# A hybrid decoder layer on one core: the prologue with rstd in diagonal matrices, state-major tables, and the first product tile begun inside the second half of x

## The reference

```python
xn = rmsnorm(x, norm_g)                       # x * rsqrt(mean(x^2) + 1e-6) * g
proj = xn @ w_in                              # 2048 -> 10240: u_a, z_a, q, k, v, z_b, g_a, g_b
# S5 branch, per group g (64) and state n (64):
dt = exp(log_dt)[:, None]; a_bar = exp(lam * dt)      # lam = A_re + i A_im
b_bar = ((a_bar - 1) / lam) * (B_re + i B_im)
h_t = a_bar * h_{t-1} + b_bar u_t;  y = Re(C h) + D u
# stick-breaking attention on q, k, v; both branches gated, merged, @ w_out, final rmsnorm
```

## Time and profile before

| | us |
|---|---|
| median of 3 runs | 3260.21 |
| lowest, highest | 3258.67, 3263.64 |
| the profiled execution | 3258.7 |
| its span, first to last instruction | 3256.9 |
| PE busy in the span | 3124.3 (96%) |
| DVE, ACT, POOL busy | 1006.6, 997.6, 760.1 |

### The profile page before, as it was taken

The page is one execution under the profiler, slowest core; times in us unless marked ns, Lnnn a source line. Parts: engine busy times, 40 slices in busy tenths (PEclk is TensorE's granted clock), DMA queues, the critical chain, the costliest instruction groups (busy, mean ns, idle before and its releaser), DMA issues.

```text
span 3256.9 us, 50354 instructions
## 1 busy us (share of the span) xinstructions
PE 3124.3 (96%) x20212; PEld 3043.6 (93%) x20212; DVE 1006.6 (31%) x1345; ACT 997.6 (31%) x1258; POOL 760.1 (23%) x2309
## 2 busy tenths in 40 slices
PE   4999999999999999999999999999899999999997
PEld 4999999899999989999998999999899999999997
DVE  5113213311321331132133113212465214332265
ACT  5215313521531352153144215314522101121142
POOL 5550360055036005404600540450012000000000
PEclk8999999999999999999999999999999989999999
DMA  5221222122122212212221221222348545342283
GB/s 151 56 90 58 61 67 80 57 56 92 55 61 68 79 60 57 91 53 62 67 79 61 65 83 53 63 66 79 118 135 272 194 150 176 98 136 71 65 243 107
DMA packets 395720, 304.05 MB, mean 93 GB/s; under 512 B 57250, under 2 KB 364018, under 8 KB 393458
## 3 DMA queue, kind: packets, MB, share of 16 engines
q1 hardware_dynamic: 395506, 301.02, 30.2%
HBM read 227.27 MB, written 65.27 MB: 90 GB/s over the span
## 4 chain that ended last, share of the span: by engine, by line
PE 84%; POOL 5%; ACT 3%; DVE 3%; issue 2%; SPq 1%; DMA 1%; POOLq 0%; DVEq 0%; ACTq 0%
PE acc L1635 71%; PE side L1596 5%; PE side L1775 2%; PE side L1828 1%; PE side L1770 1%; ACT L790 1%; DMA t_oz<-work 1%; ACT stage L790 1%; DVE work L1402 1%; POOL prologue L1039 1%; POOL work L1147 0%; DVE work L1412 0%; POOL work L1149 0%; POOL work L1148 0%; POOL work L1150 0%
## 5 line engine op out<-in xcount | busy, mean ns | idle before, releaser
L1635 PE MATMUL acc<-x_high,w_high 128*128 128x344 f32 (+2 forms) x5440 | 1229.4, 329 | 17.8 <-issue 9.9
L1635 PE MATMUL acc<-x_low,w_high 128*128 128x344 f32 (+2 forms) x5440 | 1186.0, 321 | 0.0
L1635 PE MATMUL acc<-x_high,w_low 128*128 128x344 f32 (+2 forms) x5440 | 1181.6, 321 | 0.0
L1635 PEld LDWEIGHTS acc<-x_high,w_high 128*128 128x128 f32 x5440 | 915.3, 190 | 43.1 <-issue 32.4
L1635 PEld LDWEIGHTS acc<-x_low,w_high 128*128 128x128 f32 x5440 | 928.1, 190 | 0.0
L1635 PEld LDWEIGHTS acc<-x_high,w_low 128*128 128x128 f32 x5440 | 918.5, 189 | 0.0
L1321 DVE TENSOR_TENSOR w_low<-w_raw,w_high 128x1024 fp32r<-128x1024 f32 x233 | 290.7, 1248 | 1052.2 <-ACT w_high L796 1052.1
L796 ACT CAST w_high<-w_raw 128x1024 fp32r<-128x1024 f32 x232 | 243.0, 1047 | 1008.3 <-PE acc L1635 937.1
L1137 POOL COPY work<-s_tables 128x28 f32 x16 | 8.6, 536 | 1385.9 <-DMA work<-t_state_seeds 1385.9
L1596 PE MATMUL side<-work 128*128 128x128 f32 (+6 forms) x832 | 152.7, 308 | 9.7 <-DVE work L1388 9.7
L1596 PEld LDWEIGHTS side<-work 128*128 128x128 f32 (+3 forms) x832 | 100.2, 159 | 43.0 <-issue 25.6
(11 more groups left out here) (287 smaller groups left out, 2517.4 us busy)
## 6 DMA issues: line engine op xcount, KB each, us to landing
w_raw<-in_w_in SPq DMA_DIRECT2D x160, 512.0 KB, 3.8
w_raw<-in_w_out SPq DMA_DIRECT2D x48, 512.0 KB, 4.0
work<-t_sig_ga SPq DMA_DIRECT2D x24, 516.0 KB, 4.5
out<-work SPq DMA_DIRECT2D x18, 512.0 KB
t_sig_gb<-stage SPq DMA_DIRECT2D x16, 516.0 KB, 4.2
t_qk<-stage SPq DMA_DIRECT2D x16, 516.0 KB, 4.9
work<-t_qk SPq DMA_DIRECT2D x16, 516.0 KB, 3.7
t_sig_ga<-stage SPq DMA_DIRECT2D x16, 516.0 KB, 4.2
```

The lines of the kernel that those rows point to most:

```text
L1635: ins = mm(acc[s][:, a, 0:n], w[b][:, kk, :], x[:, kx, c0:c0 + n], start=start, stop=stop)
```

## The change

- DVE no longer scales x. For each row block it writes a 128 x 128 matrix with rstd on the diagonal (`diag`, over the second high weight buffer), and the step on PE is a product of the block's columns with that matrix in place of a transpose.
- log_dt is loaded to all 128 partitions (broadcast) and A_re, A_im ahead of x block 1; PE transposes A right away; time steps, tables and angle are computed on 128 partitions, state-major, and the seven tables are written to `tab` where they are used. The fourteen table transposes, ACT's copy and the semaphores `tp_ready`, `par_t`, `tab_ready` are gone. The denominator moves behind the second pair of norms.
- `first_tile` on PE: after 21 of 32 steps it does the first 344 columns of chunk 0 of the first output tile, one feature tile between two steps; then C's transposes, the last three steps, the S transposes, the other 688 columns of chunk 0, and chunk 1. The steps of the second half use five banks. The loop over i is turned by eight steps.
- ACT and DVE split chunk 0 between the halves; `squares` and `x_high` are interleaved 3, 3, 2 in place of 2, 3, 4.

```diff
+        sp.dma_start(T[3], log_dt[0:1, :].to_broadcast([P, GROUPS])).then_inc(dt_in, 16)
+        sp.dma_start(A_rows[:, 0:64], A_re[0]).then_inc(par_in, 16)
+        sp.dma_start(A_rows[:, 64:128], A_im[0]).then_inc(par_in, 16)
         load_x(1)
-        sp.dma_start(tp[:, 0:64], A_re[0]).then_inc(par_in, 16)
-        sp.dma_start(tp[:, 64:128], A_im[0]).then_inc(par_in, 16)
-        sp.dma_start(tp[:, 128:129], log_dt.rearrange("a g -> g a")).then_inc(par_in, 16)
...
-        for n in range(9, 24):
+        for n in range(8, KT):
             x_high(n)
         act.wait_ge(raw_loaded[0], 16)
         nc.scalar.copy(hi[0][:, :, :], raw[0][:, :, :]).then_inc(hi_ready, 1)
-        for n in range(24, 2 * KT):
+        for n in range(KT, 2 * KT):
             x_high(n)
-        act.wait_ge(par_t, 1)
-        nc.scalar.copy(tab[:, :, :], side[:, 0, 0:7 * GROUPS].rearrange("p (a g) -> p a g", a=7)).then_inc(tab_ready, 1)
         act.wait_ge(seed_mm, 1)
...
-        def scale(n):
-            V.tensor_scalar(x_block(n), x_block(n), nrstd[:, NEW + n:NEW + n + 1], None, ALU.mult).then_inc(x_scaled, 1)
+        def spread(n):
+            V.tensor_scalar(diag[:, n, :], ident[:, :], nrstd[:, NEW + n:NEW + n + 1], None, ALU.mult).then_inc(x_diag, 1)
...
+        def x_transposes(n):
             half, k = n // KT, n % KT
-            if k == 0:
-                pe.wait_ge(x_scaled, 4 * half + 4)
-            if n >= 6:
-                pe.wait_ge(x_lo, n - 5)
+            prior = [m for m in range(n) if X_BANKS[m] == X_BANKS[n]]
+            if prior:
+                pe.wait_ge(x_lo, prior[-1] + 1)
             for b in range(4):
-                last = tr(acc[n % 2][:, n // 2 % 3, b * P:(b + 1) * P], x_block(4 * half + b)[:, k, :], ident[:, :])
+                if k == 0:
+                    pe.wait_ge(x_diag, 4 * half + b + 1)
+                last = one(x_bank(n)[:, b * P:(b + 1) * P], x_block(4 * half + b)[:, k, :], diag[:, 4 * half + b, :])
             last.then_inc(x_tr, 1)
...
+        def first_tile():
+            for n in range(KT + 5):
+                x_transposes(n)
+            acc_free(0, U)
+            split_ready(1)
+            pe.wait_ge(x_lo, KT)
+            for k in range(CK):
+                last_op = products(0, k, k, 0, ALL[0:1], k == 0, False)
+                x_transposes(KT + 5 + k)
+            pe.wait_ge(seed_in, 4 * 16)
+            pe.wait_ge(den_ready, 2)
+            for k in range(FT):
+                last = tr(side_flat[:, k * P:(k + 1) * P], C_in[:, k * P:(k + 1) * P], ident[:, :])
+            last.then_inc(seed_mm, 1)
+            for n in range(KT + 5 + CK, 2 * KT):
+                x_transposes(n)
+            pe.wait_ge(x_lo, 2 * KT)
+            for k in range(4):
+                last = tr(acc[1][:, 2, k * P:(k + 1) * P], S_in[:, k * P:(k + 1) * P], ident[:, :])
+            last.then_inc(seed_mm, 1)
+            for k in range(CK):
+                last_op = products(0, k, k, 0, ALL[1:], k == 0, False)
+            last_op.then_inc(chunk_used, 1)
...
-                            pe.wait_ge(tab_ready, 1)
...
         with pe.Fori(0, FT - 1) as i:
-            phase_a(i, False)
-        phase_a(FT - 1, True)
+            phase_a(i, False, range(8, PTS))
+            phase_a(i + 1, False, range(8))
+        phase_a(FT - 1, True, range(8, PTS))
```

More of the change, by code:

```diff
@@ L733, in _ @@
         act.wait_ge(pre_mm, 1)
-        nc.scalar.copy(gcol[:, :], side[:, 1, 0:KT])
+        nc.scalar.copy(gcol[:, :], side[:, 1, 0:KT]).then_inc(gcol_ready, 1)
         squares(0)
@@ L745, in _ @@
         squares(4)
-        for n in range(2):
+        for n in range(3):
             x_high(n)
@@ L749, in _ @@
         root(2, NEW + 4, NEW + 6)
-        for n in range(2, 5):
+        for n in range(3, 6):
             x_high(n)
         squares(6)
-        for n in range(5, 9):
+        for n in range(6, 8):
             x_high(n)
@@ L1025, in _ @@
         step = Chain(pool, pool_chain, 3)
-        T = [tp[:, 64 * n:64 * n + 64] for n in range(TS)]
-        dt = T[3][:, 0:1]
+        dt = T[2]
         Ar, Ai = T[0], T[1]
@@ L1259, in angle, with split_lo @@
             V.tensor_tensor(q_, hh, hh, ALU.mult).then_inc(den_ready, 1)
-        dve.wait_ge(par_in, 48)
+        dve.wait_ge(dt_in, 16)
         time_steps()
-        step(V.tensor_tensor(den, Ar, Ar, ALU.mult), V.tensor_tensor(part, Ai, Ai, ALU.mult))
-        step(V.tensor_tensor(den, den, part, ALU.add))
-        V.reciprocal(den, den).then_inc(den_ready, 1)
+        dve.wait_ge(par_mm, 1)
+        V.tensor_copy(tp[:, 0:128], side[:, 1, P:2 * P]).then_inc(den_ready, 1)
+        def split_lo(b, n1):
+            dve.wait_ge(hi_ready, n1)
+            V.tensor_tensor(lo[b][:, :, :], raw[b][:, :, :], f32(hi[b][:, :, :]), ALU.subtract).then_inc(lo_ready, 1)
         def norms(b, a, e):
@@ L1290, in _ @@
         V.tensor_tensor(sn, sn, gcol[:, :].unsqueeze(1).broadcast_to([P, NEW, KT]), ALU.mult).then_inc(xs_sq, 1)
-        angle()
         dve.wait_ge(x_sq, 4)
         norms(1, NEW + 2, NEW + 4)
-        scale(2)
-        scale(3)
+        spread(2)
+        spread(3)
+        dve.wait_ge(den_ready, 1)
+        step(V.tensor_tensor(den, Ar, Ar, ALU.mult), V.tensor_tensor(cm1, Ai, Ai, ALU.mult))
+        step(V.tensor_tensor(den, den, cm1, ALU.add))
+        step(V.reciprocal(den, den))
+        angle()
         dve.wait_ge(xs_hi, 1)
         V.tensor_tensor(XL[:, :, SEQ:TOK], snorm.rearrange("p (b f) -> p f b", f=KT), f32(XH[:, :, SEQ:TOK]), ALU.subtract)
-        for n in range(2):
+        for n in range(3):
             x_low(n)
@@ L1301, in _ @@
         norms(2, NEW + 4, NEW + 6)
-        scale(4)
-        scale(5)
-        for n in range(2, 7):
+        spread(4)
+        spread(5)
+        for n in range(3, 8):
             x_low(n)
@@ L1640, in split_ready @@
             pe.wait_ge(lo_ready, n1)
+        def first_tile():
[21 more added lines that the diff above has]
+            last_op.then_inc(chunk_used, 1)
+            split_ready(2)
+            for k in range(CK):
+                last_op = products(1, k, CK + k, 0, ALL, False, k == CK - 1)
+            last_op.then_inc(chunk_used, 1)
         def acc_free(i, t):
@@ L1654, in acc_free, with phase_a @@
                 pe.wait_ge(stage_ready[s], i * 4 + m + 1 + PRIMED)
-        def phase_a(i, last):
-            for p in range(PTS):
+        def phase_a(i, last, steps):
+            for p in steps:
                 cn = p // 4
```

99 lines of the change are left out of this document (47 added, 52 removed).

## The result

The changed kernel took 3245.78 us (median of 5 runs, 3243.69 to 3246.68), the kernel before, beside it, 3261.37 (5 runs, 3258.67 to 3267.59): a ratio of 0.9948 with an interval from 0.9933 to 0.9963. The forecast was 3253.0 and its range ended at 3247.5, so the run is faster than the range allows. The profiled run of the changed kernel took 3243.69 with a span of 3241.9, 15.0 less than the span of before. 7.1 us of gain had been forecast; 15 came. One execution of each kernel was profiled, and the executions of one kernel lie up to 17 us apart (3253.7 to 3270.6 for the kernel before), so rows show where the time goes and the medians and ratios how much it is.

The account below looks back on a forecast made before the run. PE work bounds the run outside the start; the start is bound by the seed-to-M chain over SP, DMA and GpSimd. Profiled 3258.7 - 7.1 for earlier seeds = 3251.6; median stood 1.5 higher: 3253.0 us, range 3247.5 to 3260.

Parts of the forecast that it names:

- S: Prologue: start of SP's first seed DMA, once the third seed copy is done; forecast 62.3 us, 7.1 us sooner than 69.34.
- Each us of S is a us of the run: Prologue: an earlier first seed DMA shortens the run equally, as long as PE gets to p = 9 first.
- The chain of 36.6 from S: Prologue: 36.6 us on SP, DMA and GpSimd from first seed DMA to PE's release at M1/M2 transposes, taken as unchanged.
- PE is at p = 9 by 88 and waits 11: First feature tile: PE reaches M1/M2 transposes at 88 us, release comes at 98.9, so it waits 11 us, not 6.
- a loop entry and a cold stretch: PE's path to p = 9 in the first feature tile: 1.6 us for entering the loop, 1 us for running cold.
- The seven later loop turns only move from p = 0 to p = 8 (1.55 each before), zero: PE's loop over i after the start: turns only change place, so they were costed at zero gain.
- (a): Rival, mid-start: PE's clock falls after idling, seeds 2.5 to 4.7 us later, gain 2 to 4.5, 3256 us; 27%.
- 0.9 of spare waits: Second half of x on PE: 0.9 us added for waits on high and low parts around the weight split.
- (b): Rival, x blocks on PE: each costs 1.7 us for good, seeds 15 us later than now, 3275 us; 7%.
- (c): Rival, x blocks on PE: products at 0.16 us or less, PE keeps up with VectorE, 3249 to 3247 us; 10%.
- (e): Rival, start: x block 1, log_dt or third weight chunk late, nothing within resolution, 3257 to 3260 us; 9%.
- (d): Rival, first release: wait at M1/M2 transposes does not bind, gain near 19 us, 3241 us; 2%.

## Why the prediction was wrong

**S, the first seed DMA: right.** 62.3 forecast, 61.91 measured, by the steps as they were costed: diagonals at 19.0 (19.1), a product with a diagonal at 0.22 (0.22), the end of x at 59.8 (60.1), the table transposes gone.

**Each us of S is a us of the run: right at the release, less clear in the whole.** Three runs moved S by 3.1, 3.5 and 11.2 us, and the release by 3.4, 3.1 and 9.95. The whole run followed by 6.5 to 8 us for the last; for the other two the ratios show no change. Undoing the turn leaves the prologue alone, 3253.0, which is the forecast to the tenth. That much agreement is luck: its eight runs reach from 3248.37 to 3256.9, and in its profile S was at 60.30, 1.6 us ahead of the changed kernel's with the same prologue, and 6.5 of the 10.5 us won up to the mark at i = 0 were lost again behind it. (The sum of the prediction, by its own terms, is 3253.1.)

**The chain of 36.6 from S: right within 0.7.** 35.9 here, 35.7 to 37.1 in the other kernels with the new prologue.

**PE is at p = 9 by 88 and waits 11: near.** It was there at 85.1 and waited 12.8. I had added a loop entry and a cold stretch that did not come; both would have been covered by the wait.

**"The seven later loop turns only move from p = 0 to p = 8 (1.55 each before), zero": this step failed,** and it carries the whole error of 7 us. Behind it stood the premise that outside the start nothing but PE's work counts, since PE is busy 96% of the span. (The turns are six and not seven: the page's waits of before have "issue" six times.) A turn was taken as a fixed bubble that costs the same wherever it stands. Three things are wrong with that. The stretch in which it stood was bounded by the chain over SP and GpSimd and not by PE, so its bubble at p = 0 was already hidden there. The bubble was not harmless to that chain: it lengthened it by 1.5 us, 9.8 over the seven periods. And at p = 8 it is hidden again, ahead of the wait, while at p = 12 it is not. The profile of before had the data: its line 1678 waited seven times and not once, 7.8 us beside the first (the only one in the earlier trace rows), which says that the chain binds in six of the seven later periods (in the other PE's bubble was 2.05 us and left no wait); and the last i, which stands behind the loops of SP and of PE, had its M 29.1 us after the write of t_oz, against 30.9 to 31.1 in the others. I had looked at the first release alone. The step was worth 9.8 us alone and 7 to 9 us on top of the prologue.

**The rivals.** (a), the clock falling in mid-start, happened in part. PE idled 2.4 us until 35.64, and then (stretch, length, PE busy, granted clock, DMA share, GB/s):

```profile
34.00:36.00 2.00, 0.36 (x3) 1.00 0.03 4
36.00:38.00 2.00, 2.00 (x13) 0.54 0.00 0
38.00:40.00 2.00, 2.00 (x13) 0.61 0.00 0
40.00:42.00 2.00, 2.00 (x20) 1.00 0.93 210
```

For some 3 us PE was granted the lower level, 1.2 GHz, and issued 13 operations in 2 us instead of 20; it was back before the stretch that binds, so by half the pace for 3 us I estimate its cost at 1.5 us of S at most; the forecast had 0.9 of spare waits against it. (b), a block at 1.7 for good, did not happen: the blocks stood 0.89 apart. The rule of the Trainium skill behind it (TensorE: Matmul & The Clock Gate, section Terms), that the transpose mode is four times faster for FP32, does not show in these rows: 0.22 against 0.11 is a factor of two, and undoing the diagonals gives 0.45 a block, the same factor. By the factor of four the run would have been near 3275. (c), cheap products, did not happen. (e), a late load, did not happen here; in one execution of a later kernel x's second block came 3 us late. (d), with its 3241, came out nearest in time but not in mechanism: the wait at the first release did bind. It had asked for the chain to shrink, and said that nothing in the diff touches it; the turned loop touches it, in every period but the first.

## What to carry to other kernels

Date the chain that releases the busy engine, in every period and not only in the first, before costing an edit of the busy engine at zero: a wait that is small but comes in each period says that the other chain is the bound. In this kernel a loop turn had two prices, its own bubble, which was free ahead of a wait and full behind it, and a delay of another engine's issues in the same microseconds; it pays to try turns of different engines apart, and each ahead of a wait that covers it. Before a difference of whole runs is put down to one place, take the period apart at fixed instructions and read the granted clock: here the chain explained 5 us of a change of 14. And what a start can win is the date of the transfer that releases the run: here moving twelve small transposes forward (8 us) won about as much as rebuilding the prologue around them (7 us).

## What was unexpected of the hardware

- A turn of PE's loop moved by one step (2.9 us) changed the run by +14 us, by four or eight steps by -10. Of the +14 some 5 stand on the chain in the profiled execution. In the bad place, at i = 3, SP's issue of one DMA took 1.56 us in place of 0.38, in the old place a pair took 1.96 in place of 1.06, and a 512 KB transfer landed after 3.8 and 3.3 us in place of 2.7.
- The bubble of PE's turn was 1.5 to 2.1 us at steps 0 and 12, and 0.8 to 1.4 at steps 1, 4 and 8. Why it differs was not found.
- Behind one and the same wait of 3.12 us TensorE's clock stayed up in some periods and was at 1.2 GHz for a few microseconds in others, with the same program; in the kernel before the 31.25 us up to the end of the next wait became 32.7 or 33.9.
- Products with a diagonal in fp32 run at 0.22 us per 128x128 where a transpose of the same data runs at 0.11.
- The second block of x landed between 9.7 and 10.5 in twelve profiled executions and at 12.96 in one, with no difference in the program ahead of it; that one execution was 9 us slower than the median of its kernel, of which 3.4 us (103.47 against 100.05 for the mark at i = 0) are there in the start.
